# A hybrid encoder layer: ScalarE's exponentials ahead of its copies in every attention step

## The reference

```
h = x @ w_in                                  # 1024 -> 3328 columns
A: 8 heads, rotary q and k, dilated windows   # scores, mask, exp, sum, times v
B: 8 query heads on 2 key/value heads, q and k RMS-normalised, axial rotary, dense
f = concat(A, B) * silu(gates) @ w_out
y = LayerNorm(alpha * x + f)
```

## Time and profile before

| | us |
|---|---|
| median of 3 runs | 475.52 (475.06 to 475.53) |
| the profiled execution | 475.14 |
| its span, first to last instruction | 473.3 |
| attention: first `mask_max` to the last `values` | 94.5 to 400.5 |
| busy in the span: PE, DVE, POOL, ACT | 437.3, 309.9, 232.2, 221.4 |
| mean granted TensorE clock | 0.984 |

### The profile page before, as it was taken

One profiled execution on the slowest core, in us unless ns is written; L12 is line 12 of the kernel. 1 busy time (PEld: TensorE's weight loads), 2 busy tenths in 40 slices (PEclk: granted clock), 3 DMA queues, 4 the chain that ended last, 5 costly groups with the idle time before them and its releaser, 6 DMA issues.

```text
span 473.3 us, 8952 instructions
## 1 busy us (share of the span) xinstructions
PE 437.3 (92%) x3292; PEld 412.1 (87%) x3292; DVE 309.9 (65%) x856; ACT 221.4 (47%) x507; POOL 232.2 (49%) x304
## 2 busy tenths in 40 slices
PE   1899979998899999999999999999999798999992
PEld 1899968987799999998899999999887678999992
DVE  1543675339987788654677977864686877424797
ACT  3343112335555555666565656565675776221000
POOL 1126953795544646434336565663643673454110
PEclk9999989999899999999999999999999989999998
DMA  6611212110200100202020010020100127231123
GB/s 230 263 46 50 73 37 70 43 46 23 68 24 22 47 24 24 67 24 57 13 66 24 24 46 23 24 69 24 44 24 24 44 73 284 66 114 46 44 91 133
DMA packets 23291, 30.00 MB, mean 63 GB/s; under 512 B 1872, under 2 KB 19408, under 8 KB 23248
## 3 DMA queue, kind: packets, MB, share of 16 engines
q1 hardware_dynamic: 22816, 29.30, 19.3%
q10 hardware_dynamic: 432, 0.13, 0.1%
HBM read 26.28 MB, written 3.15 MB: 62 GB/s over the span
## 4 chain that ended last, share of the span: by engine, by line
PE 65%; DVE 11%; POOL 10%; issue 7%; ACT 3%; DMA 2%; SPq 1%; DVEq 0%; POOLq 0%; ACTq 0%
PE bank L503 15%; PE bank L504 15%; PE bank L505 15%; PE bank L464 9%; PE bank L592 6%; POOL scr L1064 3%; DVE prob L863 2%; PE bank L550 2%; PE bank L551 2%; DMA cst<-consts 2%; DVE tmp_s L789 1%; POOL tanh L1050 1%; ACT prob L706 1%; POOL w_lo L1034 1%; POOL h L1081 1%
## 5 line engine op out<-in xcount | busy, mean ns | idle before, releaser
L503 PE MATMUL bank<-w_hi,t_lo 128*128 128x256 f32 x576 | 167.6, 291 | 1.9 <-DVE nmax L863 0.8
L505 PE MATMUL bank<-w_hi,t_hi 128*128 128x256 f32 x576 | 163.3, 283 | 0.0
L504 PE MATMUL bank<-w_lo,t_hi 128*128 128x256 f32 x576 | 163.3, 283 | 0.0
L503 PEld LDWEIGHTS bank<-w_hi,t_lo 128*128 128x128 f32 x576 | 110.8, 192 | 3.1 <-DVE nmax L863 1.0
L504 PEld LDWEIGHTS bank<-w_lo,t_hi 128*128 128x128 f32 x576 | 110.9, 193 | 0.1
L505 PEld LDWEIGHTS bank<-w_hi,t_hi 128*128 128x128 f32 x576 | 110.6, 192 | 0.0
L1034 POOL TENSOR_TENSOR w_lo<-raw,w_hi 128x512 fp32r<-128x512 f32 x52 | 67.3, 1303 | 59.8 <-ACT w_hi L658 59.7
L1115 POOL TENSOR_SCALAR prob<-prob,den 128x512 f32<-128x512 f32 (+1 forms) x96 | 60.5, 635 | 68.6 <-DVE den L892 68.6
L706 ACT ACTIVATE prob<-prob,nmax 128x512 f32<-128x512 f32 (+1 forms) x96 | 62.3, 649 | 53.6 <-DVE nmax L863 53.2
L871 DVE TENSOR_TENSOR p_lo<-bank,p_hi 128x512 fp32r<-128x512 f32 x80 | 54.8, 685 | 2.9 <-ACT p_hi L715 2.1
L658 ACT ACTIVATE w_hi<-raw 128x512 fp32r<-128x512 f32 x62 | 37.5, 621 | 35.0 <-DMA raw<-w_in 17.5
(11 more groups left out here) (93 smaller groups left out, 777.9 us busy)
## 6 DMA issues: line engine op xcount, KB each, us to landing
raw<-w_in SPq DMA_DIRECT2D x50, 256.0 KB, 2.8
raw<-w_out SPq DMA_DIRECT2D x16, 256.0 KB, 2.9
h<-x_prompt SPq DMA_DIRECT2D x7, 512.0 KB, 6.6
h<-x_sample SPq DMA_DIRECT2D x4, 512.0 KB, 9.7
y_prompt<-h SPq DMA_DIRECT2D x8, 256.0 KB, 2.2
y_sample<-h SPq DMA_DIRECT2D x4, 256.0 KB, 2.0
cst<-consts SPq DMA_DIRECT2D x1, 960.0 KB, 9.7
h<-x_prompt SPq DMA_DIRECT2D x2, 256.0 KB, 3.9
```

Source lines behind the costliest of these rows:

```text
L503: nc.tensor.matmul(out, a_lo, b_hi, start=(m == 0), stop=False)
L504: nc.tensor.matmul(out, a_hi, b_lo, start=False, stop=False)
L505: ins = nc.tensor.matmul(out, a_hi, b_hi, start=False, stop=(m == KT - 1))
```

## The change

In each step ScalarE issues `exps(u)` before `t_high` and `prob_high(u-3)`, and no longer behind them. The instructions, their sizes and their waits stay the same, and no other engine's order changes.

```diff
             for u in range(STEPS):
+                if u < NU:
+                    exps(u)
                 for b in steps[u]:
                     t_high(b)
                 if LAG <= u < NU + LAG:
                     prob_high(u - LAG)
-                if u < NU:
-                    exps(u)
                 for c, n in items_at(u):
                     for g in slices_at(c, n):
                         weights_high(g)
```

## The result

| | before | changed |
|---|---|---|
| median of 4 runs | 475.29 us (474.86 to 475.53) | 532.66 us (531.59 to 534.07) |
| the profiled execution | 475.14 | 532.41 |
| its span | 473.3 | 530.6 |
| mean granted TensorE clock | 0.984 | 0.956 |

The changed kernel is slower by 12.1%: ratio 1.121, 95% interval 1.1181 to 1.1239. In the profiled executions the span grew by 530.6 - 473.3 = 57.3 us. The prediction said 518 with a range of 503 to 538.

A forecast was written before the change was run, and what follows sets the result against it. The prediction took TensorE as the bound through most of the attention, VectorE second. Uncovered forced idle of 34.7 us, plus 6.3 for uneven stretches and 2 for a longer gap, made 43 on 475.14: 518 us, range 503 to 538.

The forecast's parts named there:

- The chain mask, exponential, copy, low part: In 77 attention steps VectorE idles after its mask until an exponential and a copy are through, 1.38 us or more each.
- One sign: VectorE's waits for `p_hi` were to grow from 2.1 us in 3 places to over 70 in more than 60.
- 56.5, the upper end: Highest growth of the whole time from the prediction's terms: 34.7 + 12.6 + 9.2 us.
- The size of the forced idle: On VectorE in the attention, 110.7 us over 77 steps, plus 2 us for a longer gap after the exponential.
- The cover: VectorE's earlier idle time in each attention stretch absorbs forced idle; only the excess, 34.7 us in sum, lengthens the kernel.
- the first head, which I called covered: From 94.5 to 117.7 us, two such steps: VectorE's work and forced idle make 18.2 of 23.2 us, so no growth.
- The half of 12.6 us that I took for uneven stretches: Seven steps without a projection item, in two stretches that came out even, cost up to 12.6 us; 6.3 taken.
- It stays hidden: Rival: TensorE is the bound and the three-step lag hides the later copy; about 477 us, chance 0.07.
- Faster: Rival: earlier exponentials bring reciprocal, scaling and transposes forward, ending 7.0 us of reciprocal waits; about 468 us, chance 0.03.
- The clock: Rival: TensorE's clock falls in 15 more places, none covered, adding 26 us; about 544 us, chance 0.12.

The follow-up runs named there:

- e7: Changed kernel with the exponentials of the step before, ahead of the copies; reciprocal behind the mask and scaling kept in their step: 473.96 us, ratio 0.9965.
- e4: Changed kernel with VectorE's mix moved behind the next step's mask, ahead of `prob_low`: 501.27 us, ratio 1.0557.
- e1: Changed kernel with the copies of staged queries and keys back ahead of the exponentials, only the copy of probabilities behind them: 511.49 us, ratio 1.0795.
- e6: Changed kernel with 12 extra matmuls, results unused, in steps that have values and no projection item: 534.74 us, ratio 1.1247.
- e9: Changed kernel with the new ScalarE order only in the 25 steps of heads 5 to 7 and 11 to 12, old order elsewhere: 478.77 us, ratio 1.0067.

## Why the prediction was right, and where it was short

**The chain mask, exponential, copy, low part: right.** e7 is the test: same order of kinds on ScalarE, no wait on this step's mask, and all 57 us are gone. e4 shows the same from VectorE's side. One sign was off: the waits for `p_hi` alone were 65.6 us in 43 places, not over 70 in more than 60, because in the 37 steps with a staged copy ahead of it VectorE waits for that copy (L697) instead. TensorE's idle time grew by 39.5 us, where the prediction had 43; the other 17.8 us of the growth are longer busy time of TensorE at a lower clock, which the prediction's sum did not count, and of which e1 and e6 leave room for a few microseconds of cost.

**The size: at the edge.** The growth of 57.3 us lies a little above 56.5, the upper end that the prediction's own terms gave; the range held it only because it was drawn on to 538. The two terms that fell short are these.

**The size of the forced idle: 6.6 us short.** I counted 110.7 us and added 2; the four waits say 119.3. The gap from exponential to `prob_high` is mostly the 0.84 us of the earlier trace rows, to which I gave little weight: a prompt step without a staged copy waits 1.50 us (20 of 24), a sample step 1.78 (15 of 16), instead of 1.38 and 1.66. Over these 40 steps this is 4.4 us. In the 37 steps with a staged copy the 1.38 held on average only: VectorE waited 1.15 us for a copy of 64x256 alone, 1.36 for one of 512 columns, and 1.55 where two copies stood between. I had left out the two staged copies of units 0 and 2, which wait without a `prob_low` behind them (1.37 and 1.15 us), and the last three `prob_low`, which wait 0.46 to 0.57 each for copies that no longer ran ahead.

**The cover: 9.4 us short.** VectorE was idle for 306.0 - 222.97 = 83.0 us of the attention before and for 364.95 - 222.99 = 142.0 after. Of the 142.0, 119.3 is forced, so 22.7 of the old kind stayed and 60.3 served as cover; the prediction had used 112.7 - 43 = 69.7. The two shortfalls, 6.6 and 9.4, make 16.0: the attention grew by 59.0 us against the 43 predicted; 1.6 us of that are taken back by its earlier start.

Where cover was missing: in the first head, which I called covered, 4.6 us: its long waits for GpSimd end at 102.75, and the gaps of 1.15, 1.36 and 1.64 us come behind them; in heads 13 and 14, where the sum said 6.9 and 13.7 were measured. There VectorE still waits 4.1 us for gate items, 3.5 of them in one place (to 404.28), a few microseconds after TensorE ran at its lower level (granted clock 0.50 from 392 to 398), and its own busy time is 1.4 us higher than before (25.47 against 24.04). The half of 12.6 us that I took for uneven stretches came out about right in heads 5 to 7 and 11 to 12 (5.9 + 1.0 = 6.9 us against 6.3), perhaps by luck: the same order in these heads alone cost 3.2 us (e9).

**The rivals.** *It stays hidden* fell: the cost is nearly hidden in heads 5 to 7 and 11 to 12 (e9), but those are 25 of 77 steps. *Faster* fell in the form given; a faster version exists (e7), but it needs another unit's exponentials. *The clock* fell as a large price: it went down to 0.956, in the places expected, and raising it to 0.978 (e6) gave 2.4 us in heads 13 to 15 and nothing in the whole; with the clock at 0.982 (e1) 36 us of loss remained.

## What to carry to other kernels

An instruction that is moved ahead on an in-order engine takes its wait along: ask what the wait is for, and whether the engine that gives it stands, further down its own queue, behind something you just moved back. If so, the two engines alternate instead of overlapping, and a pipeline's lag does not help, since the idle time returns every step; compare it with the idle time of the waiting engine stretch by stretch, and expect a good part of that idle time (here 23 of 83 us) not to be usable. To have work early, move it across a step boundary (here the exponentials of the unit before), so that its wait is over when the engine gets to it.

## What was not expected of the hardware

What follows a 128x512 exponential starts either 0.72 or 0.84 us after it, and the kind of instruction does not settle which. The copy of probabilities started 0.83 to 0.84 us after the exponential's start in 20 of the 24 places where it came next (256.81 to 257.65 above), but 0.72 to 0.73 in three. The staged copies of 512 columns, which read PSUM too, started after 0.71 to 0.73 in all 24 of theirs (261.33 to 262.06), those of 256 columns after 0.84 in 9 places and 0.72 in 6, and a rounding of weights, which reads SBUF, after 0.72. Why is not settled here.

The mean granted clock fell by 0.028, and raising it by 0.022 again with extra matmuls gave no shorter time on the whole. That TensorE was often not the engine that the others waited for fits this, but the price of the extra matmuls is in it too.
